# A hybrid attention and state-space layer: a latent tile's split cut in token halves and put behind an exponent, and one sum of squares put behind a row maximum

## The reference

```
u    = x * (1 + scale) + shift                  # modulation from c
proj = u @ w_in                                 # q_lat, kv_lat, k_rope, z_attn, xbc, dt, z_ssm
q    = rms_norm(q_lat) @ w_qb                   # 8 heads of 128 + 64 rotary
k, v = rms_norm(c_kv) @ w_kvb                   # latents: 384 for q, 256 for kv
o_a  = causal_softmax(q k / sqrt(192)) v * silu(z_attn)
y    = ssd(conv(xbc), dt) + xs * d_skip         # chunks of 128 tokens, 16 heads
h    = y * silu(z_ssm)
o_s  = h * rsqrt(mean(h*h, over each 512) + eps) * gain
out  = layer_norm(alpha * x + gate * (concat(o_a, o_s) @ w_out))
```

## Time and profile before

| | |
|---|---|
| median of 3 runs | 934.62 us (934.42 to 935.2) |
| profiled execution, its own time | 934.46 us |
| its span, first to last instruction | 932.6 us |
| mean granted TensorE clock | 0.996 of full speed |
| busy share: PE, VectorE, ScalarE, GpSimd | 96%, 72%, 50%, 23% |
| DMA, mean over the span | 135 GB/s |

### The profile page before, as it was taken

How to read it: one execution, slowest core, us unless ns; L and a number is a source line. 1 busy time by engine, 2 the same in 40 slices (tenths; PEclk the granted TensorE clock), 3 DMA queues, 4 the chain that set the end, 5 groups by cost and what they waited for, 6 DMA issues and landing times.

```text
span 932.6 us, 13480 instructions
## 1 busy us (share of the span) xinstructions
PE 898.0 (96%) x4737; PEld 747.7 (80%) x4737; DVE 672.0 (72%) x1078; ACT 462.3 (50%) x727; POOL 216.4 (23%) x116
## 2 busy tenths in 40 slices
PE   4999999999999999999989999999999999999995
PEld 3788778788878788877878888888888788888884
DVE  6977489966877677777656766766766758457977
ACT  3654243533544554346457667666675934323421
POOL 1022212322212122121561323413315000002412
PEclk9999999999999999999999999999999999999998
DMA  9973204411234424444660422431422549534611
GB/s 297 320 280 96 63 22 160 112 46 45 66 116 136 140 86 134 135 135 127 178 215 15 147 64 88 147 105 44 146 104 90 181 154 407 194 135 152 204 51 79
DMA packets 110044, 126.27 MB, mean 135 GB/s; under 512 B 10646, under 2 KB 84599, under 8 KB 110007
## 3 DMA queue, kind: packets, MB, share of 16 engines
q1 hardware_dynamic: 109600, 124.95, 41.5%
q10 hardware_dynamic: 406, 0.84, 0.3%
HBM read 93.98 MB, written 27.85 MB: 131 GB/s over the span
## 4 chain that ended last, share of the span: by engine, by line
PE 71%; issue 12%; DVE 6%; SPq 5%; ACT 3%; POOL 1%; DMA 1%; DVEq 0%; ACTq 0%; POOLq 0%
PE bank L856 17%; PE bank L755 13%; PE bank L757 12%; PE bank L756 12%; PE bank L994 3%; SPq L404 2%; PE bank L979 2%; PE bank L873 2%; PE bank L983 2%; PE bank L982 2%; PE bank L980 2%; PE bank L981 2%; POOL wl L664 1%; PE bank L910 1%; PE bank L875 1%
## 5 line engine op out<-in xcount | busy, mean ns | idle before, releaser
L664 POOL TENSOR_TENSOR wl<-wraw,wh 128x1024 fp32r<-128x1024 f32 x31 | 78.1, 2520 | 199.0 <-ACT wh L1182 199.0
L755 PE MATMUL bank<-uh,wh 128*128 128x512 f32 x272 | 107.9, 397 | 2.8 <-DVE ul L1534 2.2
L756 PE MATMUL bank<-ul,wh 128*128 128x512 f32 x272 | 106.1, 390 | 0.0
L757 PE MATMUL bank<-uh,wl 128*128 128x512 f32 x272 | 106.0, 390 | 0.0
L856 PE MATMUL bank<-uh,wh 128*128 128x512 f32 x256 | 102.7, 401 | 0.0
L856 PE MATMUL bank<-ul,wh 128*128 128x512 f32 x256 | 101.2, 395 | 0.0
L755 PE MATMUL bank<-owh,mxh 128*128 128x512 f32 x256 | 100.1, 391 | 0.0
L856 PE MATMUL bank<-uh,wl 128*128 128x512 f32 x256 | 99.9, 390 | 0.0
L757 PE MATMUL bank<-owh,mxl 128*128 128x512 f32 x256 | 99.7, 390 | 0.0
L756 PE MATMUL bank<-owl,mxh 128*128 128x512 f32 x256 | 99.7, 389 | 0.0
L1280 ACT ACTIVATE dec<-dec 128x512 f32<-128x512 f32 x32 | 20.3, 633 | 113.1 <-DVE dec L1695 113.1
(11 more groups left out here) (231 smaller groups left out, 2207.7 us busy)
## 6 DMA issues: line engine op xcount, KB each, us to landing
wraw<-in_w_in SPq DMA_DIRECT2D x33, 512.0 KB, 3.7
owr<-in_w_out SPq DMA_DIRECT2D x32, 512.0 KB, 4.6
wada<-in_w_ada SPq DMA_DIRECT2D x16, 512.0 KB, 6.0
dec<-acum_scratch SPq DMA_DIRECT2D x32, 256.0 KB, 3.8
proj_scratch<-ost SPq DMA_DIRECT2D x16, 512.0 KB, 4.7
xin<-in_x SPq DMA_DIRECT2D x8, 512.0 KB, 6.0
cx<-in_w_ada SPq DMA_DIRECT2D x1, 4096.0 KB, 16.7
ssm_scratch<-xd SPq DMA_DIRECT2D x8, 512.0 KB, 5.4
```

What stands on the lines that cost most here:

```text
L664: pool.tensor_tensor(wl[:, p], wraw[:, p], wh[:, p].bitcast(F32), ALU.subtract).then_inc(w_split, 1)
L755: pe.matmul(dst, ah, bh, start=start, stop=False)
L756: pe.matmul(dst, ah, bl, start=False, stop=False)
L757: return pe.matmul(dst, al, bh, start=False, stop=stop)
```

## The change

Six places in the code, two parts.

The third latent tile: ScalarE makes its high part after `exp_decay(3)` of the last chunk and not before. GpSimd subtracts its low part in two instructions, the right half of the tokens first, each counting `lat_split` up by one, so that the count after tile 2 is 4 and at the end `LAT + 1`. SP reads the last latent tile, which goes into the buffer that both halves read, at `lat_split` = 4. PE's wait for 3 now means the right half; its second unit (i = 6), which reads the left half, waits for 4, and its first key unit (i = 3) for 6.

The last sum of squares: in `ssm_tile` of the last tile GpSimd waits, between the square and the add into `sqa`, for the first row maximum of head 7 (`s_max` = 57).

```diff
--- before.py
+++ after.py
@@ -518,7 +518,7 @@
             def latent(t):
                 sp.wait_ge(w_split, 33 + t if t < 2 else 34)
                 if t >= 2:
-                    sp.wait_ge(lat_split, t - 1)
+                    sp.wait_ge(lat_split, t - 1 if t < 4 else 4)
                 sp.dma_start(wraw[:, t % 2], scr[t].rearrange("p (k n) -> p k n", n=P)).then_inc(lat_in[t % 2], 16)
 
             sp.wait_ge(stage_ready, CHUNKS)
@@ -696,8 +696,9 @@
             for t in range(LAT):
                 hi, lo = (v[:, t, :] if t < QLT else w[:, t - QLT, :] for v, w in ((qlh, ckh), (qll, ckl)))
                 pool.wait_ge(lat_hi, t + 1)
-                pool.tensor_tensor(lo, wraw[:, t % 2].rearrange("p k n -> p (k n)"), hi.bitcast(F32),
-                                   ALU.subtract).then_inc(lat_split, 1)
+                whole = wraw[:, t % 2].rearrange("p k n -> p (k n)")
+                for r in (slice(HB, S), slice(0, HB)) if t == 2 else (slice(0, S),):
+                    pool.tensor_tensor(lo[:, r], whole[:, r], hi[:, r].bitcast(F32), ALU.subtract).then_inc(lat_split, 1)
                 if t == 1:
                     weights_low(0, ROPE_W)
                 if t == 2:
@@ -710,6 +711,8 @@
                 pool.tensor_tensor(rl[:, 1, :], rl[:, 1, :], rl[:, 0, :], ALU.mult).then_inc(yg_ready, 1)
                 pool.wait_ge(yg_ready, h + 1)
                 ch.link(pool.tensor_tensor(rl[:, 0, :], rl[:, 1, :], rl[:, 1, :], ALU.mult))
+                if isinstance(h, int) and h == HEADS - 1:
+                    pool.wait_ge(s_max, 8 * h + 1)
                 pool.tensor_tensor(sqa[:, g, :], sqa[:, g, :], rl[:, 0, :], ALU.add).then_inc(sqa_ready, 1)
 
             def gain_right(s):
@@ -932,8 +935,10 @@
                 if (kind, n) == ("qn", 1):
                     pe.wait_ge(hw_split, 2 * h + 4)
                 if isinstance(h, int) and h == -1:
+                    if i == 6:
+                        pe.wait_ge(lat_split, QLT + 1)
                     if i == 3:
-                        pe.wait_ge(lat_split, LAT)
+                        pe.wait_ge(lat_split, LAT + 1)
                     if i < 2:
                         pe.wait_ge(hp_evac, 2 - i)
                 elif isinstance(h, int) and h == 0 and i >= 6:
@@ -1299,9 +1304,9 @@
                 exp_decay(2, c)
                 act.wait_ge(g_ready, 4 * c + 2)
                 exp_rows(3, c)
+                exp_decay(3, c)
                 if not more:
                     latent_high(2)
-                exp_decay(3, c)
                 act.wait_ge(arg_ready, 4 * c + 4)
                 if more:
                     act.activation(cdv[:, 2, :], cdv[:, 1, :], ACT.Exp).then_inc(dte_ready, 1)
```

## The result

The changed kernel takes 937.0 us (median of 22 runs, 934.88 to 938.82) beside 934.97 for the kernel before (22 runs, 933.92 to 938.11). The ratio is 1.0017 with a 95% interval of 1.001 to 1.0024: slower by 1.6 us by the ratio (2.0 by the medians), where 1.5 less was predicted. The sum was off by 3 us, and its sign with it. The profiled execution of the changed kernel took 936.8 us, with a span of 935.0.

A forecast was written before the change was run, and what follows sets the result against it. TensorE, busy 96% of the span, bounds the kernel, so only its waits near the two edits can move. Edit A -0.3 and edit B -1.2 give -1.5 on 934.62: 933.1 us, range 932.3 to 934.2.

The forecast's parts named there:

- The held instructions: Round 3's four VectorE arguments, held to 3.28 us by GpSimd's third latent subtract, take 1.14; PE's rope unit gains 1.2.
- The fifth latent's issue: Last SSD chunk: the fifth latent's read waits for both subtract halves, so is issued at 467.9 instead of 465.7.
- Its landing: The fifth latent's read lands 3.2 us after issue, at 471.1; PE stands 0.6 us at the first key unit.
- Slower: Rival: the fifth latent's read meets traffic and takes 1.8 us more; edit A +1.5, total 934.9 us; chance 0.05.
- The swap's landing: Rope swap of `tb` into `tc`, behind SP's stores, lands at 478.5, between 477.8 and 480.1; gain 0.3 us.
- nearer the first: The first bound of the swap's landing, 477.8: only the issue counts, pieces land 4.2 us after it; gain 1.05.
- far bound: Latest landing of the rope swap, 480.1: 3.0 us after y's store lands, as before; a loss of 1.3 us.
- The memset: GpSimd's memset of `sqa` doesn't hold VectorE's rope sum, so edit A stays at -0.3 us; otherwise +0.15.
- is hidden by the rope path: PE's 0.6 us wait at the first key unit costs nothing unless the fifth latent lands over 1.3 us later.
- Edit B: Last sum of squares, head 7: -1.5 us at the scores, +0.3 from a new gated-sum wait, -1.2 in all.
- Eaten: Rival: swap pieces wait for stores, or the memset holds the sum; edit A costs 0 to 0.8; 933.7 us; chance 0.19.
- edit A: Third latent's high copy moved behind exponent 3 and its subtract split: -0.3 us at the first scores of head 0.

The follow-up runs named there:

- the runs with the swap first: SP's half of the rope swap issued ahead of the two stores: ratio 0.9994 on the third-latent part alone, 1.0013 on the kernel before.
- the filled ones: Needless matmuls in PE's two waits: third-latent part alone 1.0017, whole change 1.0006, kernel before with the fifth latent's read late 1.0046.
- late-read kernel: Kernel before, with only the fifth latent's read made to wait for the QK weight subtract: 940.57 us, ratio 1.0061.

## Why the prediction was wrong, point by point

**The held instructions: right.** Round 3's four arguments take 1.15 us in after (at 464.44), the rotary unit gains 1.26 where 1.2 was said, and the halves end when they were said to (469.80, less 1.86, for 467.9).

**The fifth latent's issue: right.** 469.87 less 1.86 is 468.0, for 467.9.

**Its landing: mis-sized.** 3.9 us, not 3.2. That was the rival "Slower" in kind, but 0.7 and not its 1.8. ScalarE's Silu half ends at 473.5 (forecast 472.7) and PE's wait at the key unit is 1.43, not 0.6.

**The swap's landing: the step that failed.** "I take 478.5, nearer the first": the sum that waits for it starts at 482.17 less 1.86, 480.3, just past the far bound of 480.1. Of the 1.8 us, 0.8 is SP's later issue (474.4 for 473.6), which follows from the read. The other 1.0 is the landing: 5.9 us from SP's issue, where 4.9 was taken and the kernel before shows 4.2 behind stores that were nearly through. The step took the swap's own latency for all there was and set little for the overlap; the store of y took longer too (5.4 for 3.9). The first scores lose 1.5 where 0.3 was to be gained. That the far bound of 480.1 came out nearly right is luck: it was 3.0 us behind a landing of y's store at 477.1, and that store landed at 479.5 (the memset behind it starts at 481.32, less 1.86), 0.9 before the sum. The Trainium skill, page "DMA: Bandwidth & Descriptors", section "Queues, rings and completion order", says that each DMA engine takes the descriptors of a ring in order; the runs with the swap first agree for SP's pieces (2.6 us ahead of the stores, 4.9 behind them). ScalarE's pieces are not in SP's queue and slowed too (4.5 for 3.2), which that sentence doesn't explain.

**The memset: never in play.** In after GpSimd clears `sqa` from 481.32 to 483.13, and the rotary sum starts beside it. GpSimd's timeline of after:

```profile
481.32 1.81 POOL L738 MEMSET sqa<- 128x2048 f32 x1 [2.77 <-DMA ssm_scratch<-xd]
```

VectorE's:

```profile
482.17 1.23 DVE L374 TENSOR_TENSOR ta<-ta,tc 128x1024 f32<-128x1024 f32 x1 [1.79 <-DMA tc<-tb]
```

It takes 1.23 us, as in the kernel before, where nothing ran beside it. By the Trainium skill, page "SBUF — State Buffer", section "SBUF: two separate sides", only a GpSimd instruction that reads SBUF holds one with two inputs, and this row agrees.

**PE's wait at the key unit "is hidden by the rope path": wrong in what it left out.** It costs no time on the path. But with the wait before the scores it makes two stops of 1.4 and 2.2 us within some 10 us, and the clock falls in more of the executions, for about 0.7 us by the shares. The prediction priced no idle time by the clock. In the profile of after itself the granted clock is 1.00 throughout 476 to 492 us; that the waits act through the clock rests on the share of executions, on the half clock seen in place in two other kernels, and on the filled ones.

**Edit B: right.** Forecast -1.2 with a wait of 0.45 to 0.5; stretch 2 shows -1.03 and -1.14, the wait is 0.38, and -1.4 was measured. Only that 0.2 of the wait would be slack was wrong: with the wait gone the stretch is 0.48 shorter.

**The chances.** "Slower" had 0.05. It was thought of as one late read, when the edit made all of SP's queue late together; and "Eaten" named the right mechanism with its price capped at the bare gain. By the far bound that the text itself had set for the swap, edit A came to +1.3; it was given too little weight.

What stays open: some 0.4 us of the loss, which neither the two traces nor the shares of the clock hold; why ScalarE's pieces slow with the stores, and what the transfers share when they overlap. From the swap's issue to the sum it took 4.8 and 4.9 us with the stores behind it, 5.9 with both just ahead, and 4.2 with them well ahead; no run moved the stores away altogether.

## What to carry to other kernels

Moving the release of a double-buffered tile moves the next read, and with it all that the issuing queue holds behind that read: follow that queue to its end before pricing the gain at the front. A small transfer on the critical path should not stand behind large stores that can be made late; and when two orders are possible, look for which path is right behind the first. Idle time of the bottleneck engine that is "hidden" is not free when it stands next to another idle time, since the granted clock may answer; measure it over many executions, because one profile may not show it.

## What was not expected of the hardware

- Two DMA issues on SP took 3.00 us behind two stores of 512 KB (3.48 in the late-read kernel), and 1.16 when they stood ahead of them or well behind.
- PE at half clock for some 6 us of work after waits of 1.84 and 2.93 us, while busy for most of the time between; and in another kernel's profile, with waits of 1.53 and 2.11, no fall there at all.
- Executions of one kernel differ by 1.2 us with a mean clock of 0.995 or less against 0.996 or more (before: 935.94 and 934.76), so a median depends on how many are of which kind.
